# Two neighbouring cache pages share two places of the ring, each partition holding two neighbouring tokens

## What is computed

```python
def one_seq(args):
    qi, ckv_i, kpe_i, pages = args
    ckv_all = jnp.concatenate([cache_ckv[pages].reshape(past, D_LATENT), ckv_i], axis=0)   # D_LATENT 512
    kpe_all = jnp.concatenate([cache_kpe[pages].reshape(past, D_ROPE), kpe_i], axis=0)     # D_ROPE 64
    k = mla_keys(ckv_all, kpe_all, w_uk, g_k)
    sc = jnp.einsum('qhd,khd->hqk', qi, k).astype(jnp.float32) * scale
    sc = jnp.where(mask[None], sc, -jnp.inf)          # masks nothing here: the new token is the last
    p = jax.nn.softmax(sc, axis=-1).astype(ckv_all.dtype)
    o_lat = jnp.einsum('hqk,kc->qhc', p, ckv_all)
    return jnp.einsum('qhc,chv->qhv', o_lat, w_uv)
```

## Time and profile before

| | |
|---|---|
| Median of 3 timed runs | 2634.8 us (2628.03, 2634.8, 2641.3) |
| Profiled execution | 2627.88 us |
| Its span, first to last instruction | 2626.2 us |
| PE, DVE, ACT, POOL busy | 84%, 82%, 35%, 52% of the span |
| DMA queue q0 (GpSimd): packets, MB, share of 16 engines | 154704, 562.94, 55.6% |
| DMA queue q1 (SyncE) | 209498, 186.53, 23.0% |
| Page loads (ckv), issue to landing, median | 16.6 us x80, 17.0 us x48 |

### The profile page before, as it was taken

One profiled execution on the slowest core, in us unless ns is written; L12 is line 12 of the kernel. 1 busy time (PEld: TensorE's weight loads), 2 busy tenths in 40 slices (PEclk: granted clock), 3 DMA queues, 4 the chain that ended last, 5 costly groups with the idle time before them and its releaser, 6 DMA issues.

```text
span 2626.2 us, 36376 instructions
## 1 busy us (share of the span) xinstructions
PE 2201.2 (84%) x11497; PEld 1571.4 (60%) x11497; DVE 2156.1 (82%) x4009; ACT 917.3 (35%) x3596; POOL 1353.3 (52%) x1209
## 2 busy tenths in 40 slices
PE   5999998997989988687999999999999889963232
PEld 3999998884448854344665656565656556642020
DVE  3775688995555326988999999999999989999797
ACT  3331101333252003213445454555454545441110
POOL 0221231112002103776777777777777777777574
PEclk8999999998999999798999999999999989985666
DMA  6334877455007767999999999999999999999997
GB/s 207 98 85 128 217 216 195 130 157 158 13 16 221 217 203 263 388 396 400 403 396 381 406 384 404 374 402 375 401 366 399 382 392 408 363 406 396 400 403 276
DMA packets 385726, 776.49 MB, mean 296 GB/s; under 512 B 50473, under 2 KB 200058, under 8 KB 385497
## 3 DMA queue, kind: packets, MB, share of 16 engines
q0 software_dynamic: 154704, 562.94, 55.6%
q1 hardware_dynamic: 209498, 186.53, 23.0%
q10 hardware_dynamic: 21332, 24.70, 2.9%
HBM read 744.85 MB, written 29.37 MB: 295 GB/s over the span
## 4 chain that ended last, share of the span: by engine, by line
DVE 25%; issue 15%; DMA 12%; PE 6%; POOL 4%; ACT 1%; SPq 0%; DVEq 0%; POOLq 0%; ACTq 0%
DVE mix_pair L2655 11%; DVE mix_u L2754 9%; DMA mix_u<-in_peer_u,mix_ids 7%; DMA chs_wq<-in_peer_wq 3%; PE mix_pair L2199 2%; POOL mix_v L2157 2%; POOL mix_u L2150 2%; PE mix_pair L2256 2%; PE mix_pair L2167 1%; DMA pag_kpe<-in_cache_kpe 1%; DMA keep_x<-mix_sc 1%; DMA mix_v<-in_peer_v,mix_ids_half 1%; PE mix_pair L2276 0%; DMA mix_u<-in_peer_u,mix_ids_half 0%; DVE mix_s L1829 0%
## 5 line engine op out<-in xcount | busy, mean ns | idle before, releaser
L2256 PE MATMUL mix_pair<-pag_wx,pag_ckvT 128*128 128x384 f32 (+3 forms) x3072 | 945.4, 462 | 17.4 <-ACT mix_pair L2466 12.3
L2256 PEld LDWEIGHTS mix_pair<-pag_wx,pag_ckvT 128*128 128x128 f32 x3072 | 579.8, 194 | 314.9 <-issue 23.3
L2157 POOL DMA_INDIRECT mix_v<-in_peer_v,mix_ids x512 | 618.2, 1207 | 182.4 <-issue 169.9
L2150 POOL DMA_INDIRECT mix_u<-in_peer_u,mix_ids x512 | 550.0, 1074 | 268.2 <-issue 145.3
L2754 DVE CUSTOM_DVE_ANT_0 mix_u<-mix_u,mix_h 128x1024 f32<-128x1024 f32 x512 | 621.6, 1214 | 52.4 <-DMA mix_u<-in_peer_u,mix_ids 50.7
L2655 DVE SCALAR_TENSOR_TENSOR mix_pair<-mix_v,mix_coef,mix_pair 128x1024 f32<-128x1024 f32 x508 | 650.4, 1280 | 1.3 <-DMA mix_v<-in_peer_v,mix_ids 1.3
L2466 ACT ACTIVATE mix_pair<-mix_pair 128x128 f32<-128x128 f32 x1024 | 269.2, 263 | 316.7 <-PE mix_pair L2256 316.5
L373 PE MATMUL inp_ps<-inp_h_hi,inp_w_hi 128*128 128x260 f32 x1168 | 340.1, 291 | 21.5 <-DVE inp_w_lo L367 14.4
L375 PE MATMUL inp_ps<-inp_h_hi,inp_w_lo 128*128 128x260 f32 x1168 | 333.7, 286 | 0.0
L374 PE MATMUL inp_ps<-inp_h_lo,inp_w_hi 128*128 128x260 f32 x1168 | 333.3, 285 | 0.0
L407 POOL CAST inp_w_hi<-inp_w 128x1024 fp32r<-128x1024 f32 x73 | 88.8, 1216 | 374.7 <-DMA inp_w<-in_w_in 314.6
(11 more groups left out here) (540 smaller groups left out, 3209.8 us busy)
## 6 DMA issues: line engine op xcount, KB each, us to landing
inp_w<-in_w_in SPq DMA_DIRECT2D x72, 512.0 KB, 4.6
pag_ckv<-in_cache_ckv SPq DMA_DIRECT2D x80, 256.0 KB, 16.6
mrg_w_ada<-in_w_ada SPq DMA_DIRECT2D x16, 1024.0 KB, 8.5
all_shared<-in_cache_ckv SPq DMA_DIRECT2D x48, 256.0 KB, 17.0
chs_wq<-in_peer_wq SPq DMA_DIRECT2D x11, 1024.0 KB, 20.1
keep_proj<-stp_out ACTq DMA_DIRECT2D x32, 260.0 KB, 3.8
stp_st<-in_state_ssm POOLq DMA_DIRECT2D x8, 1024.0 KB, 7.5
out_ssm_s<-stp_st POOLq DMA_DIRECT2D x8, 1024.0 KB, 6.7
```

The lines of the kernel that those rows point to most:

```text
L2150: pool.indirect_dma_start(u[:, x % UR, :], None, u_rows, bass.IndirectOffsetOnAxis(at, 0)).then_inc(u_in[x % UR], 16)
L2157: pool.indirect_dma_start(v[:, y % VR, :], None, v_rows, bass.IndirectOffsetOnAxis(at, 0)).then_inc(v_in[y % VR], 16)
L2256: last = pe.matmul(to, ckvT[:, g % 2, k, :], wx[:, k, lo:hi], start=(k == 0), stop=(k == KL - 1))
```

## The change

A pair of pages `g`, `g + 1` (`g` even) now fills its two places together. Page `g` goes to partitions 0 to 63 of both places and page `g + 1` to partitions 64 to 127 of both. Partition `p` of a half holds tokens `2p` and `2p + 1` of its page, the even one in the first place and the odd one in the second. So a page's `ckv` is read as 64 rows of 4 KB and its `kpe` as 64 rows of 512 B. What is read from a place later (transposes, squares, scores, weighted sum) is as it was; each place holds half of the tokens of either page.

```diff
+TOGETHER = 2
...
+        page_group = lambda r: (ckv[:, r:r + TOGETHER, :] if r < NPG - SHARED else ckv_shared[:, r - (NPG - SHARED):r - (NPG - SHARED) + TOGETHER, :]).rearrange("p r c -> p (r c)")
+        rope_group = lambda g: o_raw[:, g * ROPE:(g + TOGETHER) * ROPE] if g < SHARED else kpe[:, ring(g):ring(g) + TOGETHER, :].rearrange("p r c -> p (r c)")
...
             def load_page(g):
                 page = sp.value_load(table[0:1, g:g + 1], min_val=0, max_val=A["cache_ckv"].shape[1] - 1)
-                sp.dma_start(page_rows(ring(g)), A["cache_ckv"][0, bass.ds(page, 1)].rearrange("a p c -> (a p) c")).then_inc(page_in[ring(g) // 4], 16)
-                sp.dma_start(rope_rows(g), A["cache_kpe"][0, bass.ds(page, 1)].rearrange("a p c -> (a p) c")).then_inc(page_in[ring(g) // 4], 16)
+                first, at = g - g % TOGETHER, slice(g % TOGETHER * PAGE // TOGETHER, (g % TOGETHER + 1) * PAGE // TOGETHER)
+                sp.dma_start(page_group(ring(first))[at, :], A["cache_ckv"][0, bass.ds(page, 1)].rearrange("a (p n) c -> (a p) (n c)", n=TOGETHER)).then_inc(page_in[ring(g) // 4], 16)
+                sp.dma_start(rope_group(first)[at, :], A["cache_kpe"][0, bass.ds(page, 1)].rearrange("a (p n) c -> (a p) (n c)", n=TOGETHER)).then_inc(page_in[ring(g) // 4], 16)
```

## The result

| | before | changed |
|---|---|---|
| Median of the timed runs | 2635.4 us (2628.03 to 2641.3, 4 runs) | 2775.9 us (2772.76 to 2782.3, 4 runs) |
| Ratio | | 1.0543, 95% interval 1.0517 to 1.0568 |
| Profiled execution, its span | 2627.88, 2626.2 us | 2773.55, 2771.9 us |

A forecast was written before the change was run, and what follows sets the result against it. DMA and VectorE were taken as both full. 128 pages at 0.80 us gave 102 us, less 8 us for packets and 38 us taken up by dips: 56 us slower, 2691 us, range 2632 to 2755 us.

The forecast's parts named there:

- The rows of an earlier stage: Loads ahead of the attention: 422 GB/s with a 128-partition load nearly alone, 211 GB/s with only 32- and 64-partition loads.
- fewer packets: Page loads: 16,384 packets fewer at 7.7 ns each over 16 engines, at most 8 us of DMA time saved.
- The packets' case: Rival on the page loads: partitions don't matter, only packet count does, DMA work falls by 8 us; 2627 us, chance 0.06.
- the price of a page: Page loads to half the partitions: 0.80 us more DMA work per page, 102 us for 128 pages.
- a bound, 1.2 us: Upper price per page if gathers beside it suffer as much: 0.82 MB at 250 instead of 397 GB/s.
- the mixed row: Loads ahead of the attention, partial transfers beside `q_n`: 250 GB/s, 2.33 us lost to 0.75 MB, giving 0.92 us per page.
- the 38 us of the dips: DMA idle time in eight dips, one per sequence, between 1320 and 2410 us; expected to take up 38 us of new work.
- the thirteen places: Rings of six and seven buffers holding up to thirteen gathers, named in favour of slack taking the extra DMA work; chance 0.12.
- the far end of a rival: Gathers suffer too, at 1.2 us a page: 108 us, 2743 us; with dips staying, 146 us, 2781 us; chance 0.12.
- TensorE's waits for pages: Seven waits, 26.9 us in total, taken as first pages behind a sequence's end; cost nothing, or 27 us more if not covered.
- The page queue's time per packet: Sign in a burst: some 175 ns per packet of 2060 B if doubled, 87 ns for no effect of the partitions.
- VectorE's waits for `u`: Sign at VectorE's waits for gathered rows: 49.8 us before, growing by roughly 50 us.

The follow-up runs named there:

- e5: Changed kernel with four pages sharing four places, each page in 32 partitions in a row, rows of 8 KB: 2772.3 us, ratio 1.0534 to before.
- e2: Changed kernel with the even page in every second partition from 0 and the odd page from 1, rows still 4 KB: 2633.0 us, ratio 1.0013 to before.
- e6: Changed kernel with four pages sharing four places, each page in every fourth partition, rows of 8 KB: 2630.7 us, ratio 0.9997 to before.
- e3: Changed kernel with even pages in partitions 32 to 95, odd ones in 0 to 31 and 96 to 127 by two transfers: 2708.8 us, ratio 1.0301.
- e1: Kernel before with each page load cut into two transfers of 64 partitions, rows still 2 KB and 256 B: 2732.7 us, ratio 1.0391.
- e4: Changed kernel, each page from page 9 on also waiting until TensorE is done with the page eight before it: 2733.4 us, ratio 1.0385 to before.
- e7: Kernel before, each page from page 9 on also waiting until TensorE is done with the page eight before it: 2615.7 us, ratio 0.9951.

## Why the prediction was wrong

**Right: what bounds, the cause and the direction.** DMA and VectorE were both full, the half transfers slowed the DMA, and the slowdown reached the end as VectorE's waits for gathered rows. The rows of an earlier stage foretold it. The rule of the Trainium skill ("SBUF — State Buffer", "Door 1: The DMA port swizzle") agrees with each form that was tried: 0 to 63 and quarters in a row are slow (e5), spread ones are not (e2, e6), and 32 to 95 are not if the odd pages of e3 paid what they paid. No run here sees a port; what is shown is which partitions are slow.

**Right in size, wrong in effect: fewer packets.** I put 8 us at most on it. e2 has the whole of that part without the other and is 2.5 us slower than before, ratio 1.0013; e6 has more of it and is equal. The 8 us of DMA time are there (9 us in the table above, 14 us in e6), but they went into deeper dips and not to the end. The packets' case, by which the time would have been 2627 us, and the batching rule of the Trainium skill's "Perfetto Trace Analysis" ("DMA Optimizations") behind it found nothing here: the burst's rate rose from 397 to 403 and 411 GB/s, and the end didn't move.

**Wrong, first term: the price of a page, 0.80 us.** In the changed kernel's burst, 10.70 MB took 40 us; at the 397 GB/s of before they take 26.95 us. The 13.05 us lost fall to 3.57/0.295 = 12.1 pages: 1.08 us each. That window is among the dearest: windows inside six bursts (1445 to 1495, 1605 to 1645, 1770 to 1795, 1930 to 1965, 2085 to 2125, 2245 to 2285 us) give 0.87 to 1.10 us, 0.99 us in the mean. I had such a case as a bound, 1.2 us from the 250 GB/s of the mixed row, and went below it, because I charged the mixed row's loss to the bytes of the partial transfers alone. The gathers' packets beside them are slowed by the same 1.5, and in a burst there are more gather bytes than page bytes. The nearest row was the mixed one with all of its traffic. For pages that come one by one my figure was right: from 1260 to 1310 us the queues moved 18.05 MB, 44.9 us' worth at the 402 GB/s of the earlier trace rows, with 1.87 MB of pages, so 5.1 us for 6.3 pages, 0.80 us each. So 24 x 0.80 + 104 x 0.99 = 122 us, which is also what the table has, 144 - 22 us while the engines were full. The forecast had 102 - 8 = 94 us. (By the same table the 2 KB packets of e1 cost 104/128 = 0.81 us a page.)

```profile
DMA packets 5428, 18.05 MB, mean 361 GB/s; under 512 B 688, under 2 KB 1076, under 8 KB 5424
q0 software_dynamic: 4434, 16.14, 88.7%
q1 hardware_dynamic: 990, 1.87, 14.4%
```

**Wrong, second term, and the larger miss: the 38 us of the dips.** I wrote that a debt that grows past the dips keeps the queue from ever resting. The debt can't grow past the rings. In a burst the gathers get 7.10 MB in 40 us, 178 GB/s, where VectorE in the earlier trace rows was fed 6.17 MB in 20 us, 309 GB/s, and still ran from what lay in the rings. Once they are empty, VectorE stands (26.83 of 40 us busy), and its standing is time lost there. Behind the burst, 1655 to 1722 us, q0 brought 27.34 MB while VectorE took 23 slots of 1.05 MB, 24.1 MB (360 GB/s); the 3.2 MB between them filled the rings, and the dip came as before. The same size comes out of the other end: the burst's first page is issued at 1596 us, VectorE is full until about 1612 us and then stands, and 16 us at 360 - 178 GB/s are 2.9 MB.

```profile
1605.00:1610.00 5.00, 5.00 (x23) 3.43 (x22) 5.00 (x12) 1.40 (x11) 3.78 (x5) 1.00 1.05 268
1615.00:1620.00 5.00, 4.01 (x10) 2.75 (x11) 2.58 (x5) 1.00 (x4) 3.08 (x4) 0.50 1.05 269
```
```profile
q0 software_dynamic: 7511, 27.34, 102.6%
```

So the rings carried some 3 MB, about six gathers, of the thirteen places (6.8 MB) that I named in the prediction; a burst of 40 to 50 us that is short by 180 GB/s asks for 7 to 9 MB. Such a debt doesn't fit even into the 6.8 MB, and is two to three times the measured 3 MB. That this is the mechanism is shown by its parts: the dips in the changed kernel are deeper and not smaller, the half dose costs 54% (e3), and spreading the pages takes 42 us away (e4) and gains on the kernel before as well (e7). In the profiled executions e4's stretch is 28 us shorter than the changed kernel's, and 24 of them are dips filled, 3 a lower loss while full.

**The sum with both terms mended:** 122 us in place of 94, and 14 us of deeper dips in place of 38 us taken up, is 136 us, what the profiled stretch lost; the medians are 141 us apart. With 1.2 us a page and the dips untouched the prediction had it as the far end of a rival, 146 us, 2781 us, and gave that no weight of its own. That this lies near the 2776 us is in part luck: its price was too high and its dips too shallow. The range ended at 2755 us.

**The other steps.** TensorE's waits for pages, costed at nothing, rose from 26.9 to 33.6 us; that they cost nothing fits e2, which cut them to 7.8 us and won nothing. The page queue's time per packet was expected at some 175 ns for 2060 B and was 120 ns for 1859 B: not twice the straight line but 1.5 times, and the gathers' packets by as much. VectorE's waits for `u` were expected at some 100 us and were 199.3 us.

## What to carry to other kernels

Before a load is spread over fewer partitions, ask which ones: here 64 or 32 in a row at one side cost 0.8 to 1.1 us per 0.295 MB beside other traffic, and the same number spread evenly cost nothing, by one slice. When a slow transfer shares the engines with others, price it by all the traffic that runs beside it. And idle time of a resource is slack only for work that lies in it or that a buffer can carry there: compare the debt of a burst with what the rings carry, here about half of their places, and if it doesn't fit, spread the burst. The same holds for a saving: DMA time that is saved inside a burst came back here as a deeper dip.

## What was not expected of the hardware

A packet of the other queue, to all partitions, slows as much as the one that causes it: 224 against 148 ns, while its own was at 120 against 80. And the engines reach full rate with every second partition (403 GB/s) and every fourth (411 GB/s), no less than with all 128 in a row (397 GB/s). Long packets to one side are worse than short ones: 0.95 against 0.81 us per page over the whole stretch, although e1, with the short ones, issues twice as many transfers.
